# The first modulation vector as matmul rows in four column groups, and a first projection that follows it pair by pair

## The reference, cut to what matters

```python
def modulation(c, w, b):
    return jnp.split(jax.nn.silu(c) @ w + b, 3, axis=-1)          # w is 1024 x 3072

def sandwich(x, mod, g_pre, g_post, fn):
    shift, scale, gate = mod
    h = rms_norm(x, g_pre) * (1.0 + scale[:, None]) + shift[:, None]
    return x + gate[:, None] * rms_norm(fn(h), g_post)

# the first layer's fn begins with one large projection
u, qr, fr, vr, gr = jnp.split(h @ hyb_w_in[j], split_at, axis=-1)
```

## Time and profile before

| | us |
|---|---|
| median of 3 runs | 2723.29 |
| the profiled execution's own time | 2723.45 |
| its span | 2721.4 |
| TensorE busy | 2642.4 (97%) |
| TensorE weight loads | 2146.5 (79%) |
| VectorE busy | 1211.6 (45%) |
| ScalarE busy | 973.1 (36%) |
| GpSimd busy | 924.2 (34%) |

### The profile page before, as it was taken

One profiled execution on the slowest core, in us unless ns is written; L12 is line 12 of the kernel. 1 busy time (PEld: TensorE's weight loads), 2 busy tenths in 40 slices (PEclk: granted clock), 3 DMA queues, 4 the chain that ended last, 5 costly groups with the idle time before them and its releaser, 6 DMA issues.

```text
span 2721.4 us, 36028 instructions
## 1 busy us (share of the span) xinstructions
PE 2642.4 (97%) x14078; PEld 2146.5 (79%) x14078; DVE 1211.6 (45%) x2033; ACT 973.1 (36%) x1397; POOL 924.2 (34%) x224
## 2 busy tenths in 40 slices
PE   8999999999999989999999899999998999999997
PEld 7887788887788877888877678888876767888886
DVE  6566543343521235101259853605443564360543
ACT  3354522222533344222244743212234774321222
POOL 2322243434222223444343034444432112444442
PEclk9999999999999999999999999999999999999999
DMA  7531344543222212222222022322221112222221
GB/s 312 186 140 66 120 156 147 191 173 105 80 79 70 70 47 78 95 93 105 83 88 78 16 86 95 106 93 93 97 82 51 43 48 70 93 99 102 93 93 62
DMA packets 44031, 270.92 MB, mean 100 GB/s; under 512 B 5071, under 2 KB 8679, under 8 KB 15752
## 3 DMA queue, kind: packets, MB, share of 16 engines
q1 hardware_dynamic: 39888, 265.71, 27.8%
q10 hardware_dynamic: 4024, 3.54, 0.6%
HBM read 267.09 MB, written 2.13 MB: 99 GB/s over the span
## 4 chain that ended last, share of the span: by engine, by line
PE 67%; issue 23%; POOL 5%; DVE 4%; ACT 2%; POOLq 0%; ACTq 0%; DVEq 0%
PE lin L726 20%; PE lin L728 19%; PE lin L727 19%; POOL wlo L675 5%; PE lin L1263 1%; PE bank L1247 1%; PE bank L1273 1%; PE bank L1432 0%; DVE small L2937 0%; DVE tmp L3085 0%; PE lin L868 0%; PE bank L885 0%; DVE pt L2951 0%; PE bank L1412 0%; PE lin L1412 0%
## 5 line engine op out<-in xcount | busy, mean ns | idle before, releaser
L675 POOL TENSOR_TENSOR wlo<-raw,whi 128x2048 fp32r<-128x2048 f32 (+3 forms) x212 | 918.7, 4333 | 1761.1 <-ACT whi L1754 1761.1
L726 PE MATMUL lin<-hhi,whi 128*128 128x512 f32 x1976 | 783.9, 397 | 11.6 <-ACT projected L2249 2.6
L728 PE MATMUL lin<-hhi,wlo 128*128 128x512 f32 x1976 | 771.1, 390 | 0.0
L727 PE MATMUL lin<-hlo,whi 128*128 128x512 f32 x1976 | 770.7, 390 | 0.0
L1754 ACT ACTIVATE whi<-raw 128x2048 fp32r<-128x2048 f32 (+3 forms) x212 | 383.2, 1808 | 934.7 <-PE lin L728 871.4
L726 PEld LDWEIGHTS lin<-hhi,whi 128*128 128x128 f32 x1976 | 371.9, 188 | 103.8 <-issue 13.4
L726 PE MATMUL lin<-ghi,whi 128*128 128x512 f32 x1120 | 438.3, 391 | 3.2 <-POOL wlo L675 1.2
L728 PE MATMUL lin<-ghi,wlo 128*128 128x512 f32 x1120 | 436.0, 389 | 0.0
L727 PE MATMUL lin<-glo,whi 128*128 128x512 f32 x1120 | 435.8, 389 | 0.0
L728 PEld LDWEIGHTS lin<-hhi,wlo 128*128 128x128 f32 x1976 | 371.6, 188 | 78.9
L727 PEld LDWEIGHTS lin<-hlo,whi 128*128 128x128 f32 x1976 | 372.1, 188 | 75.1 <-issue 1.2
(11 more groups left out here) (472 smaller groups left out, 2777.6 us busy)
## 6 DMA issues: line engine op xcount, KB each, us to landing
raw<-in_w SPq DMA_DIRECT2D x171, 1024.0 KB, 4.9
adw_a<-in_ada SPq DMA_DIRECT2D x30, 1024.0 KB, 5.0
adw_b<-in_ada SPq DMA_DIRECT2D x18, 1024.0 KB, 6.7
raw<-in_w SPq DMA_DIRECT2D x20, 768.0 KB, 4.3
raw<-in_w SPq DMA_DIRECT2D x16, 640.0 KB, 3.9
raw<-in_w SPq DMA_DIRECT2D x5, 512.0 KB, 3.4
x<-in_x SPq DMA_DIRECT2D x1, 2048.0 KB, 17.0
out<-x SPq DMA_DIRECT2D x8, 256.0 KB, 2.0
```

Of the source, the lines that this page charges most:

```text
L675: nc.gpsimd.tensor_tensor(wlo[:, slot, 0:size], raw[:, slot, 0:size], whi[:, slot, 0:size].bitcast(F32), ALU.subtract).then_inc(s.wlo_ok, 1)
L726: pe.matmul(dst, lh, rh, start=first, stop=False)
L727: pe.matmul(dst, lh, rl, start=False, stop=False)
L728: return pe.matmul(dst, ll, rh, start=False, stop=last)
```

## The change: what it does

The modulation units are multiplied by PE alone and the other way round: silu(c), one column of it for each of the eight chunks of the sum, repeated 32 times, is the weight, and the 256 columns of the unit move. Chunk c of the sum goes to the group of 32 partitions c % 4. A unit is 8 program matmuls, and first_rows(p), with the shift unit and the scale unit of one pair of chunks, 16. The result is rows of 512 numbers in each group. DVE copies the bank to tmp, and PE turns rows into columns and adds the four groups in one step (first_columns: four matmuls with tmp as weights and a column that is 1 on partitions 0, 32, 64 and 96). DVE then adds the biases and the factor (first_mods).

```diff
+FIRST_ADA = (0, 4, 1, 5, 2, 6, 3, 7)
...
+            first_vecs = VEC["norm_post"][0]
+            load(vecs[:, 0:first_vecs], a["vecs"][:, 0:first_vecs], s.c_in)
             load(cst[:, 0:2 * P], a["cst"][:, 0:2 * P], s.ones_in)
-            for k in range(4):
+            load(x[:, :, :], a["x"], s.x_in)
+            unit(0, offs[0], UNIT)
+            for k in FIRST_ADA:
                 load(ada_first[k][:, :], ada_unit(k), ada_first_in[k])
...
             unit(1, offs[1], UNIT)
...
-            ring(8)
-            sp.wait_ge(s.ada_read, 1)
-            load(adw_b[1][:, :], ada_unit(9), ada_b_in[1])
+            n.up(s.ada_acc, 4)
+            for k in range(2):
+                sp.wait_ge(s.rows_mm, FIRST_ADA.index(6 + k) + 1)
+                load(adw_b[k][:, :], ada_unit(8 + k), ada_b_in[k])
...
+            def first_rows(p):
+                bank = B4 if p else B5
+                for half in range(2):
+                    k = FIRST_ADA[2 * p + half]
+                    pe.wait_ge(ada_first_in[k], 16)
+                    for c in range(DC):
+                        b = 32 * (c % 4)
+                        mm = pe.matmul(bank[b:b + 32, 256 * half:256 * half + 256], silu_c[:, c:c + 1].broadcast_to([P, 32]),
+                                       ada_first[k][:, c * 256:(c + 1) * 256], start=(c < 4), stop=(c >= 4))
+                    mm.then_inc(s.rows_mm, 1)
+            def first_columns(p):
+                pe.wait_ge(s.ada_acc, n.up(s.ada_acc))
+                for i in range(4):
+                    mm = pe.matmul((B4 if p else B5)[:, i:i + 1], tmp[:, p % 2, i * P:(i + 1) * P], one_per_row,
+                                   start=True, stop=True)
+                mm.then_inc(s.ada_mm, 1)
+            def first_sums():
+                for c in range(DC):
+                    feature_sum(c)
+                keep_busy(4, LB[3])
+                first_rows(0)
+                first_columns(0)
+                root_rows()
+                keep_busy(4, LB[3])
...
+                for c in range(DC):
+                    pe.wait_ge(s.h_ok, h0 + c + 1)
+                    for t in range(TT):
...
+                        mm = three(LB[t][:, 0:256], hi[:, tk], lo[:, tk], whi[:, 0, at], wlo[:, 0, at], c == 0, c == DC - 1)
...
+                    if c % 2 == 0 and c < 6:
+                        first_rows(c // 2 + 1)
+                    elif c < 6:
+                        first_columns(c // 2 + 1)
...
+            def first_mods(p):
+                bank, shift, scale = (B4 if p else B5), mods[:, 0, 2 * p:2 * p + 2], mods[:, 0, 8 + 2 * p:10 + 2 * p]
+                v.wait_ge(s.rows_mm, 2 * p + 2)
+                v.tensor_copy(tmp[:, p % 2, :], bank[:, :]).then_inc(s.ada_acc, 1)
+                v.wait_ge(s.ada_mm, n.up(s.ada_mm) + 2)
+                v.tensor_tensor(shift, bank[:, 0:2], vec("ada_b", 2 * p, 2), ALU.add).then_inc(s.dv, 1)
+                chain(v.tensor_tensor(scale, bank[:, 2:4], vec("ada_b", 8 + 2 * p, 2), ALU.add))
+                n.up(s.dv)
+                v.wait_ge(s.dv, n.at(s.dv))
+                chain(v.scalar_tensor_tensor(scale, scale, 1.0, vec("norm_pre", 2 * p, 2), ALU.add, ALU.mult))
...
-            for i, k in enumerate((0, 1, 3, 4, 5, 6)):
-                ada_products(ada_first[k], ada_first_in[k], i, B6, acc_first)
...
+            first_mods(0)
+            recip()
+            rows_in()
+            for p in range(4):
+                for c in (2 * p, 2 * p + 1):
+                    scaled_chunk(0, c)
+                for c in (2 * p, 2 * p + 1):
+                    low_part(c, (B5, B6), mods[:, 0, c:c + 1])
+                if p < 3:
+                    first_mods(p + 1)
```

More of the change, by code:

```diff
@@ L237, in program @@
         rsum = nm.rearrange("p a b -> p (a b)")
-        acc_first, acc = (q.rearrange("p (a n) -> p a n", a=2) for q in (tmp[:, 0, :], rstd[:, :]))
+        acc = rstd[:, :].rearrange("p (a n) -> p a n", a=2)
+        one_per_row = small[:, 61:62]
         assert base[0] <= nc.sbuf_usable_end, (base[0], nc.sbuf_usable_end)
@@ L568, in unit @@
                 load(raw[:, slot, 0:size], a["w"][bass.ds(off, P * size)].rearrange("(p n) -> p n", p=P), s_raw[slot])
-            load(vecs[:, 0:8], a["vecs"][:, 0:8], s.c_in)
+            first_vecs = VEC["norm_post"][0]
+            load(vecs[:, 0:first_vecs], a["vecs"][:, 0:first_vecs], s.c_in)
             load(cst[:, 0:2 * P], a["cst"][:, 0:2 * P], s.ones_in)
-            for k in range(4):
+            load(x[:, :, :], a["x"], s.x_in)
+            unit(0, offs[0], UNIT)
+            for k in FIRST_ADA:
                 load(ada_first[k][:, :], ada_unit(k), ada_first_in[k])
[L574 to L580, removed]
             unit(1, offs[1], UNIT)
+            load(vecs[:, first_vecs:NVEC], a["vecs"][:, first_vecs:NVEC], s.vecs_in)
             load(wpool[:, :], a["wpool"], s.pool_in)
@@ L761, in fm_unit, with tok_unit @@
                         after(t)
-            def tok_unit(slot, tile0, kc, wid, col0, cols, xs, chunks=None):
+            def tok_unit(slot, tile0, kc, wid, col0, cols, xs):
                 def part(t, c):
@@ L770, in part @@
                                  wlo[:, slot, at:at + cols], c == 0, c == kc - 1)
[L772 to L781, removed]
                 for t in range(TT):
@@ L1006, in sums, with tokens @@
                         ada_sum(k % 2, 2 * k)
-                def tokens(chunks=None):
+                def tokens():
                     pe.wait_ge(s.wlo_ok, n.up(s.wlo_ok))
-                    tok_unit(st.u % 2, st.tile, DC, 256, 0, 256, hin, chunks)
+                    tok_unit(st.u % 2, st.tile, DC, 256, 0, 256, hin)
                     st.u, st.tile = st.u + 1, st.tile + 4
@@ L1724, in _ @@
             pe.wait_ge(s.silu_ok, 1)
-            ada_sums_first()
+            first_sums()
             pe.wait_ge(s.bias_ok, 3)
-            pe.wait_ge(s.vecs_in, 16)
             hgrn_mixer()
@@ L2517, in rows_in @@
                 v.wait_ge(s.rr_mm, n.up(s.rr_mm))
[L2519 to L2525, removed]
-                low_part(DC - 1, (B5, B6), mods[:, ls, DC - 1:DC])
             def scaled_chunk(ls, c):
```

44 lines of the change are left out of this document (14 added, 30 removed).

## The result

The changed kernel took 2731.36 us (median of 7 runs, 2729.20 to 2737.93), beside 2722.97 for the kernel before (7 runs, 2721.22 to 2724.71): a ratio of 1.0035, 95% interval 1.0025 to 1.0045, so 8.4 us slower. A second set of runs gave 2732.62 beside 2723.11, 1.0031 [1.0019, 1.0042]. The forecast was 2735.0, slower. The profiled execution took 2730.45 us, with a span of 2728.7 against 2721.4 before: +7.3 us.

The account below looks back on a forecast made before the run. TensorE, busy 97% of the span, was taken as the bound. Start -11.9, round trips per pair +18.3 and clock +5.1 gave +11.5 us on 2723.45: 2735.0 us, slower, range 2727 to 2746.

Parts of the forecast that it names:

- The start: Up to TensorE's first projection matmul: it begins at 31.0 instead of 42.86 us, a gain of 11.9 us.
- The bounds of the start: First projection matmul: between 30.0 and 34 us, depending on the clock at root_rows and the keep_busy behind it.
- The rows: first_rows on TensorE: 32 instructions, four column groups side by side, take 2.0 us at the full clock.
- The Trainium skill's rule on weight loads: first_rows' weight loads: column groups share them, so four first_rows would cost 3.4 us more, sum 2738.
- The ring: First projection unit: TensorE and VectorE wait on each other for each pair, 9.0 us a pair, three times, +18.3 us.
- The clock: TensorE in the first unit's pairs: clock falls to the lower level in each, 1.7 us three times, +5.1 us.
- the shift: Everything behind the start of the second projection unit: each piece moves later by the same amount.
- What costs nothing: Later loads (units 8 and 9, third weight unit, mask) and ScalarE's second-weight split: covered by other work, no added time.
- The clock holds: Rival: TensorE's clock doesn't fall in the pairs' 3.2 us waits; +5.9 us, 2729; chance 0.16.
- The other side: Rival, not slower: VectorE's part hides, a pair costs TensorE's 5.83 us alone; -3.5 us, 2720; chance 0.09.

Follow-up runs that it names:

- e_all_first: Changed kernel with all four pairs' rows and columns ahead of the first norm, nothing between the first projection's chunks; 2722.78 us, 0.9999 of the kernel before.
- e_order_only: Kernel before with only the load order changed: x and the first weight unit ahead of the modulation units, VectorE still summing; 2729.90 us, ratio 1.0030.
- e_rows_twice: Changed kernel with the rows of the last three pairs multiplied twice; 2741.62 us, 1.0075 of the kernel before.
- e_ahead: Changed kernel with the same work, but each pair's rows and columns placed one pair earlier; 2721.70 us, 0.9998 of the kernel before.
- e_port: Changed kernel, modulation one pair earlier, reciprocal and root spreading first, ScalarE's second-weight split one chunk later, scale's first sum in PSUM; 2721.20 us, 0.9992 of kernel before.
- e_best: Changed kernel with modulation one pair earlier, reciprocal and root spreading ahead of the first rows; 2722.13 us, 0.9995 of the kernel before.

## Why the prediction was right, by its own steps

**The start: -11.9, measured -12.3.** Each step of the start came within a microsecond of its forecast (x at 11.55 for 11.1, rows at 21.15 for 21.0, the first projection at 30.54 for 31.0). One detail was another: the first matmul was not released by VectorE. It follows the second filler (L858), which ran at the lower level, 0.44 us apiece; in the second profile VectorE's low part does release it, at 30.58. The bounds of the start, 30.0 and 34, are not what the prediction's own terms give (30.5, and 35.3 with root and filler at the lower level). Both did run at the lower level, and the start was 30.54 all the same: the filler lies beside VectorE's norm. e_all_first and e_order_only show the two halves of the step: the sums by TensorE allow it, the load order alone moves the start to 50.66, 7.8 us later than before.

**The rows: 2.0, measured 1.93.** Four groups run side by side, weight loads inside. The Trainium skill's rule on weight loads ("TensorE: Matmul & The Clock Gate", section "Part 3: Packing small matmuls — row/col tiling") would have had 3.4 us more for the four, by an estimate from its page; 1.73 us for 32 further instructions in e_rows_twice don't show it. In the changed kernel's trace the next four loads start at 32.56 us, beside the first four matmuls, which started at 32.54 and end at 32.94.

**The ring: 9.0 a pair, measured 8.86 at the full level.** TensorE stood 2.89 us three times; the forecast had 3.17 with its wake-up. The three pairs took 28.2 us where they had taken 9.0: +19.2. Without the clock it is three times 8.86 less 9.0, +17.6, for the forecast +18.3. Half of that distance is the pair after, 8.86 instead of 9.0 us; the other half is the 2.88 us that the prediction took for a pair before (its unit of 11.5 us doesn't fit its own 42.86 to 54.95, which is 12.1). e_ahead moves one term of the ring, the rows, a pair ahead, and 5.4 of 8.7 us of waits go and with them the loss. That settles the cause.

**The clock: +5.1, measured +3.1 in the first profile and some +6.0 in the second.** From the pairs less 8.86 each, and the last two chunks less the 3.1 us that they took before: 0.4 + 1.3 + 1.4 in the first; 2.9 + 1.6 + 1.6 in the second. The sign and the place were right; the size is that of one draw, and the median of the first runs, 2731.36, corresponds to a smaller one than forecast. Here lies most of the distance between 2735.0 and what was measured: the sum was +8.3 at the unit's end (-12.3 + 19.2 + 1.4) in the first profile and +11.3 in the second, which is the longest of its seven runs; the forecast was +11.5, the median +8.4 in one set of runs and +9.5 in the other. Behind the unit the shift did not stay the same, as forecast. In the first profile it falls to 6.8 us behind the stretch at the lower level that was at 109 us, which stands at 119 and is 6.8 us long instead of 10.2; it is 7.3 at 270, falls to 5.7 at 700, since the stretch that was at 676 is gone, and rises to 7.2 behind a new one of 3.4 us at 976.

**What costs nothing** did so: neither the second weight unit nor units 8 and 9 end a wait ahead of 66 us.

**The rivals.** "The clock holds" (2729) is contradicted by the windows, though the first median lies nearer to its number (2.4 above) than to the forecast (3.6 below). The other side, a pair under 7.0 us, was not this kernel, but it can be had: e_ahead and e_port are that rival, with pairs of 5.8 us where nothing stood in the way. The prediction gave 2720 for it, and e_port measured 2721.20; that is partly luck, since its second unit came 6.5 us sooner than in the kernel before, not 3.5, and half of that was lost again behind it.

## What to carry to other kernels

Work that passes from one engine to another and back once per block belongs one block ahead of its use: the ring cost 2.89 us of a 97% busy engine each time, and a move of two calls took away 5.4 of its 8.7 us, while the start that the change won was worth nothing with the ring in place. Time won at the front need not arrive at the end: of e_port's 6.5 us, 1.9 went in a single wait for a weight unit 400 us later. When a long GpSimd instruction may lie beside VectorE's, look at the short VectorE instructions with both operands in SBUF on the critical path, and give them an operand in PSUM. And fill a short wait of TensorE that stands behind one-column work with a few matmuls nobody needs, if a free bank is at hand at once.

## What the runs showed of the hardware that I had not expected

- A 128x2 instruction on VectorE took 0.16 us, and 2.96 and 2.97 us when it lay beside GpSimd's 4.54 us, ending with it; with one operand from PSUM 0.16 us beside the same work. By the Trainium skill, "SBUF — State Buffer", section "Who interferes with whom", the two engines share a pair of ports that is locked for one of them at a time, and an instruction of VectorE outside its two-port modes needs it only with two inputs in SBUF. By that rule, the trace agrees; being small doesn't spare an instruction from it. In e_ahead and e_best too it lay beside such a GpSimd instruction, took 1.21 us and ended 0.03 us behind it.
- Three unused matmuls, 1.54 us, in a wait of 1.46 us that followed one-column matmuls kept TensorE at 2.4 GHz; the medians were 3.6 us less in one kernel and 8.4 in another, of which about 5 are the filler's in the profiles. Of the twelve profiles without this filler, eleven have a stretch of 6.8 or 10.2 us at the lower level there, and of the two with it none. The fall isn't certain, though: in e_ahead the same wait, as long, was followed by none, and its 20.5 us at the lower level is the shortest of all.
- Two profiles of the changed kernel differ by 10.3 us in time at the lower level. Half of that, 5.1, is about their difference in span, 4.0. A change of this kernel under some 4 us can't be read from one profile; the medians of 5 to 11 runs could.
